# Four narrow projections with high and low weights side by side in one stationary operand

## The reference

```
aq, ak, av, bq, bkv, biq, bik, biw, cq, ck, cv, g = split_cols(u @ w_in[l])      # bik: 32 columns, biw: 8
s_idx = relu(einsum('bqhd,bkd->bqhk', iqb, ik)); score = einsum('bqhk,bqh->bqk', s_idx, iwb) * idx_scale
conv_val, conv_gate, z, xbc, dt = split(x @ even_w_in)                            # dt: 16 columns
q, k, v, g_out, g_low = split(x @ odd_w_in); log_g = log_sigmoid(g_low @ w_gate2 + b_gate) / 16   # g_low: 16 columns
```

## Time and profile before

| what | value |
|---|---|
| runs | 2524.91, 2529.27 and 7747.51 us, median 2529.27 |
| profiled execution, its own time | 2532.69 us |
| its span, first to last instruction | 2531.0 us |
| granted TensorE clock, mean | 0.997 |
| PE busy | 2479.7 us, 98%, 15181 matmuls |
| DVE busy | 1702.8 us, 67% |
| ACT busy | 1294.4 us, 51% |
| POOL busy | 405.1 us, 16% |
| HBM read | 247.99 MB, 99 GB/s over the span |

### The profile page before, as it was taken

One profiled execution on the slowest core, in us unless ns is written; L12 is line 12 of the kernel. 1 busy time (PEld: TensorE's weight loads), 2 busy tenths in 40 slices (PEclk: granted clock), 3 DMA queues, 4 the chain that ended last, 5 costly groups with the idle time before them and its releaser, 6 DMA issues.

```text
span 2531.0 us, 38409 instructions
## 1 busy us (share of the span) xinstructions
PE 2479.7 (98%) x15181; PEld 2158.2 (85%) x15181; DVE 1702.8 (67%) x3249; ACT 1294.4 (51%) x2558; POOL 405.1 (16%) x476
## 2 busy tenths in 40 slices
PE   7999999999999999999999999999999999999998
PEld 6876677899988978888897999889898897999888
DVE  5476977688863499997774988534735744988533
ACT  4365544367742435554654687424534453677422
POOL 2233342200000155543010100000000100100000
PEclk9999999999999999999999999999999999999999
DMA  9432234434443233212431343333321441333332
GB/s 285 134 93 71 66 99 125 131 94 125 117 128 98 77 100 100 59 59 92 126 87 48 91 116 111 92 96 86 90 78 34 127 132 53 89 110 108 92 98 86
DMA packets 455092, 253.29 MB, mean 100 GB/s; under 512 B 16458, under 2 KB 449310, under 8 KB 454911
## 3 DMA queue, kind: packets, MB, share of 16 engines
q1 hardware_dynamic: 451615, 243.18, 33.6%
q0 software_dynamic: 3152, 7.59, 1.3%
q10 hardware_dynamic: 144, 0.07, 0.0%
HBM read 247.99 MB, written 2.80 MB: 99 GB/s over the span
## 4 chain that ended last, share of the span: by engine, by line
PE 85%; DVE 9%; ACT 3%; issue 1%; DMA 1%; SPq 1%; POOL 0%; DVEq 0%; ACTq 0%; POOLq 0%
PE ps L1134 15%; PE ps L1142 15%; PE ps L1136 15%; PE ps L1199 4%; PE ps L1201 4%; PE ps L1204 4%; PE ps L1049 4%; PE ps L1051 4%; PE ps L1047 4%; PE ps L1375 1%; PE ps L1065 1%; PE ps L1718 1%; PE ps L1740 1%; PE ps L1067 1%; PE ps L1232 1%
## 5 line engine op out<-in xcount | busy, mean ns | idle before, releaser
L1948 ACT ACTIVATE wh<-w_f 128x512 fp32r<-128x512 f32 (+2 forms) x621 | 351.0, 614 | 337.1 <-PE ps L1142 157.1
L2912 DVE TENSOR_TENSOR w_r<-w_f,wh 128x512 fp32r<-128x512 f32 (+1 forms) x459 | 295.8, 688 | 334.5 <-ACT wh L1948 333.9
L1134 PE MATMUL ps<-XH,wh 128*128 128x512 f32 (+1 forms) x1136 | 457.9, 403 | 4.5 <-ACT wh L1948 3.5
L1136 PE MATMUL ps<-XL,wh 128*128 128x512 f32 (+2 forms) x1016 | 397.8, 392 | 0.2 <-DVE XL L3432 0.2
L1142 PE MATMUL ps<-XH,w_r 128*128 128x512 f32 (+2 forms) x1160 | 310.4, 391 | 1.0 <-DVE w_r L2912 0.8
L1136 PE MATMUL ps<-arena_r,wh 128*128 128x512 f32 (+1 forms) x808 | 296.5, 373 | 0.1
L4211 POOL TENSOR_TENSOR w_r<-w_f,wh 128x256 fp32r<-128x256 f32 (+1 forms) x314 | 236.3, 782 | 353.9 <-ACT wh L1948 353.7
L1134 PEld LDWEIGHTS ps<-XH,wh 128*128 128x128 f32 (+1 forms) x1136 | 211.8, 186 | 67.6 <-issue 15.1
L1142 PEld LDWEIGHTS ps<-XH,w_r 128*128 128x128 f32 (+2 forms) x1160 | 216.1, 186 | 51.4 <-DVE w_r L2912 3.2
L1136 PEld LDWEIGHTS ps<-XL,wh 128*128 128x128 f32 (+2 forms) x1016 | 189.3, 186 | 43.1 <-issue 1.9
L1134 PE MATMUL ps<-arena_r,wh 128*128 128x512 f32 (+1 forms) x568 | 210.2, 378 | 0.8 <-ACT wh L1948 0.8
(11 more groups left out here) (505 smaller groups left out, 5964.2 us busy)
## 6 DMA issues: line engine op xcount, KB each, us to landing
w_f<-in_mlp_w SPq DMA_DIRECT2D x126, 512.0 KB, 4.0
w_f<-in_w_ff SPq DMA_DIRECT2D x63, 512.0 KB, 4.1
w_f<-in_w_in SPq DMA_DIRECT2D x49, 512.0 KB, 3.8
w_f<-in_ada_w SPq DMA_DIRECT2D x35, 512.0 KB, 3.9
w_f<-in_even_w_in SPq DMA_DIRECT2D x35, 512.0 KB, 3.8
w_f<-in_odd_w_in SPq DMA_DIRECT2D x23, 512.0 KB, 3.8
w_f<-in_even_w_out SPq DMA_DIRECT2D x16, 512.0 KB, 4.0
w_f<-in_xa_w_v SPq DMA_DIRECT2D x16, 512.0 KB, 3.3
```

What stands on the lines that cost most here:

```text
L1134: e.matmul(b, hi[:, k, :], xh, start=u.first and k == 0, stop=False)
L1136: e.matmul(b, hi[:, k, :], xl, start=False, stop=False)
L1948: e.activation(high_flat(u)[:, s], flat(u, 0)[:, s], ACT.Copy).then_inc(act.sem, act.up("high", u.n, i))
L2912: e.tensor_tensor(low[:, s], raw_[:, s], high[:, s], ALU.subtract).then_inc(dve.sem, dve.up("low", u.n, i))
```

## The change

Where a projection has at most 40 columns, its high and its low weights are put beside each other in the 128 (or 64) columns of one stationary operand. One matmul then gives both products: of the high weights in the first half of the output rows, of the low weights in the second half. Two matmuls per chunk are left, by the high and by the low input, 16 a unit. (The product of low weights and low input is computed too.) The two halves are added later, by a product with a matrix that holds ones at both places.

- `ik` and `iw` become one unit `ikw` of 40 columns (32 and 8) that stand at 0 and at 64 of 128. It takes `ik`'s place (step 13 of differential attention). Its turn yields `iw`, and a second fp32 product with `ik_pick` yields `ik` four times; both at step 15, after that step's unit.
- `dt` stands at 0 and 32 of 64 columns; its turn is a product with `dt_pick` in place of a transpose.
- `low` stands at 0 and 32 of 64 columns; `wg2` holds its 16 rows twice, at partitions 0 and 32, with zeros between, and is loaded by two DMAs after a memset.
- The low part of these units is made by DVE. `ikw` and `dt` were POOL's before.
- One unit fewer is left for differential attention: `cq 0` moves to step 14, and every later unit up to `branch 1` moves up by one: index step 0 has `ck 1`, 1 `gate 0`, 2 `gate 1`, 3 `branch 0`, 4 `gate 2`, 5 `branch 1`. Block attention's step 0, which had `branch 1`, has none; from step 2 on the units are the ones of before.

```diff
+def side_by_side(name, dram, x, beside, wide):
+    u = Unit(name, 0, dram, x)
+    u.beside, u.wide = beside, wide
+    return u
...
-    ik = Unit("ik", 0, [w_in[:, COL_IK:COL_IK + IDX_DIM]] * 4, "X0")
-    iw = Unit("iw", 0, [w_in[:, COL_IW:COL_IW + 8]], "X0")
+    ikw = side_by_side("ikw", [w_in[:, COL_IK:COL_IK + IDX_DIM], w_in[:, COL_IW:COL_IW + 8]], "X0", 2 * IDX_DIM, 4 * IDX_DIM)
...
-        plans["diff", i] = [next(fill)] if i % 4 and i < 15 else []
-        plans["diff", i] += [next(qk)] if i >= 15 else []
+        plans["diff", i] = [next(fill)] if i % 4 and i < 14 else []
+        plans["diff", i] += [next(qk)] if i >= 14 else []
...
-        plans["moba", i] = [next(fill)] if i % 3 != 1 or i == 16 else []
+        plans["moba", i] = [next(fill)] if i and i % 3 != 1 or i == 16 else []
...
-    plans["ev gv"].insert(1, Unit("dt", 0, [even[:, EV_DT:EV_DT + SSM_HEADS]], "X3"))
+    plans["ev gv"].insert(1, side_by_side("dt", [even[:, EV_DT:EV_DT + SSM_HEADS]], "X3", 2 * SSM_HEADS, 4 * SSM_HEADS))
...
-    plans["gla low"] = [Unit("low", 0, [odd[:, OD_LOW:OD_LOW + GLA_RANK]], "X7")]
+    plans["gla low"] = [side_by_side("low", [odd[:, OD_LOW:OD_LOW + GLA_RANK]], "X7", 2 * GLA_RANK, 4 * GLA_RANK)]
...
-        u.low = "pool"
+        u.low = "dve" if u.beside else "pool"
...
+        def side(u, low):
+            a = high_slots[u.high][:, 0:KC * u.wide].rearrange("p (k c) -> p k c", k=KC)
+            return a[:, :, low * u.beside:low * u.beside + u.cols]
+        def standing(u, k):
+            return high_slots[u.high][:, k * u.wide:(k + 1) * u.wide]
...
-                        if u.name == "iw":
-                            last = e.matmul(b[:, j * 8:(j + 1) * 8], g[0:8, j * P:(j + 1) * P], ident[0:8, 0:8],
+                        if u.name == "ikw":
+                            w.wait_ge(dve, "ikw picks")
+                            last = e.matmul(b[:, j * 8:(j + 1) * 8], g[:, j * P:(j + 1) * P], iw_pick, start=True, stop=True)
+                        elif u.name == "dt":
+                            w.wait_ge(dve, "dt pick")
+                            last = e.matmul(b[:, j * 16:(j + 1) * 16], g[0:u.wide, j * P:(j + 1) * P], dt_pick[0:u.wide, :],
                                             start=True, stop=True)
-                        elif u.name == "dt":
-                            last = e.transpose(b[:, j * 16:(j + 1) * 16], g[0:16, j * P:(j + 1) * P], ident[0:16, 0:16])
+                    if u.name == "ikw":
+                        b, freed = att_now[0].take("ik")
+                        w.wait_ge(*freed)
+                        e.matmul(b[:, :], ik_pick, g, start=True, stop=True).then_inc(pe.sem, pe.up("ik turn"))
...
+            def wide_products(u):
+                b = bank_of(u)[0:u.wide, :]
+                after_long[0] = True
+                w.wait_ge(act, "high", u.n, 0)
+                w.wait_ge(dve, "low", u.n, 0)
+                for k in range(KC):
+                    xh, xl = chunk_of(u, k)
+                    w.wait_ge(act, "xh", u.x, k)
+                    e.matmul(b, standing(u, k), xh, start=k == 0, stop=False)
+                    w.wait_ge(dve, "xl", u.x, k)
+                    last = e.matmul(b, standing(u, k), xl, start=False, stop=k == KC - 1)
+                last.then_inc(pe.sem, pe.up("unit", u.n))
...
                 run(("diff", i))
+                if i == 15:
+                    flush()
...
-                e.matmul(b[:, :], wg2[0:GLA_RANK, hd * P:(hd + 1) * P], low[0:GLA_RANK, :], start=True, stop=True).then_inc(
+                e.matmul(b[:, :], wg2[0:4 * GLA_RANK, hd * P:(hd + 1) * P], low[0:4 * GLA_RANK, :], start=True, stop=True).then_inc(
...
+                        if u.beside:
+                            w.wait_ge(act, "high", u.n, 0)
+                            e.tensor_tensor(side(u, 1), chunks(flat(u, 0), u.kc, u.cols), side(u, 0).bitcast(F32),
+                                            ALU.subtract).then_inc(dve.sem, dve.up("low", u.n, 0))
+                            continue
...
+            e.tensor_tensor(ik_pick.rearrange("p (a b) -> p a b", a=4),
+                            ident[:, 0:IDX_DIM].unsqueeze(1).to_broadcast([P, 4, IDX_DIM]),
+                            ident[:, 2 * IDX_DIM:3 * IDX_DIM].unsqueeze(1).to_broadcast([P, 4, IDX_DIM]), ALU.add).then_inc(
+                dve.sem, dve.up())
...
-            e.dma_start(wg2[0:GLA_RANK, :], A["odd_w_gate2_2"][0]).then_inc(d_wg2.sem, d_wg2.up("wg2", by=16))
+            e.memset(wg2[0:4 * GLA_RANK, :], 0.0).then_inc(pool.sem, pool.up("wg2 zero"))
+            w.wait_ge(pool, "wg2 zero")
+            for r in (0, 2 * GLA_RANK):
+                e.dma_start(wg2[r:r + GLA_RANK, :], A["odd_w_gate2_2"][0]).then_inc(d_wg2.sem, d_wg2.up("wg2", by=16))
```

More of the change, by code:

```diff
@@ L246, in __init__ @@
         self.low, self.halved, self.k0 = "dve", apart, 0
+        self.beside = self.wide = None
         self.paired, self.high_after, self.shift = None, None, HALF_SHIFT
+def side_by_side(name, dram, x, beside, wide):
+    u = Unit(name, 0, dram, x)
+    u.beside, u.wide = beside, wide
+    return u
 class Step:
@@ L855, in program @@
                   ("xq", 0): qT, ("xq", 1): qT, "oq": q_, "ok": k_}
-        TURNED = ("iw", "dt")
+        TURNED = ("ikw", "dt")
+        ik_pick, iw_pick, dt_pick = lamb[:, P + 64:2 * P + 64], lamb[:, 2 * P + 64:2 * P + 72], soft[:, 48:48 + SSM_HEADS]
         RESIDUAL = {"wo": "r0", ("ff2", 0): "r1"}
@@ L1292, in run_units @@
                         group = [u, steps.pop(0)] if u.pair else [u]
-                        products(group)
+                        if u.beside:
+                            wide_products(u)
+                        else:
+                            products(group)
                         for v in group:
@@ L1946, in round_to @@
                             w.wait_ge(pe, "unit", u.high_before.n)
+                        if u.beside:
+                            e.activation(side(u, 0), chunks(flat(u, 0), u.kc, u.cols), ACT.Copy).then_inc(
+                                act.sem, act.up("high", u.n, 0))
+                            continue
                         for i, s in pieces(u, HIGH_PIECE):
@@ L1957, in flush @@
                     w.wait_ge(pe, "turn", u.name, u.m)
-                    if u.name == "iw":
+                    if u.name == "ikw":
                         copy(iw, b[:, 0:32].rearrange("p (a b) -> p a b", a=NT), "iw",
                              scale=IDX_HEADS ** -0.5 * IDX_DIM ** -0.5)
+                        w.wait_ge(pe, "ik turn")
+                        copy(ik, att_now[0].of("ik")[:, :], "ik", 0)
+                        att_now[0].free(act, "ik")
                     elif u.name == "dt":
@@ L2104, in evacuate @@
                     w.wait_ge(pe, "unit", u.n)
-                    copy(g[0:u.cols, 0:u.tokens], b, "turned", name, m)
+                    copy(g[0:u.wide, 0:u.tokens], lin.of(*u.out)[0:u.wide, 0:u.tokens], "turned", name, m)
                     lin.free(act, *u.out)
@@ L2108, in evacuate @@
                     turned.append(u)
-                elif name in ("kv", "ik", "low"):
+                elif name == "kv":
                     w.wait_ge(pe, "unit", u.n)
-                    copy({"kv": kvT, "ik": ik}.get(name, low[0:GLA_RANK, :]), b, name, m)
+                    copy(kvT, b, name, m)
+                    lin.free(act, *u.out)
+                elif name == "low":
+                    w.wait_ge(pe, "unit", u.n)
+                    copy(low[0:u.wide, :], lin.of(*u.out)[0:u.wide, :], name, m)
                     lin.free(act, *u.out)
@@ L3247, in vector_program @@
             e.tensor_scalar(gbh[:, :], columns("gate_b", 0, 24), 0.5, None, ALU.mult).then_inc(dve.sem, dve.up("gbh"))
+            e.tensor_tensor(ik_pick.rearrange("p (a b) -> p a b", a=4),
+                            ident[:, 0:IDX_DIM].unsqueeze(1).to_broadcast([P, 4, IDX_DIM]),
+                            ident[:, 2 * IDX_DIM:3 * IDX_DIM].unsqueeze(1).to_broadcast([P, 4, IDX_DIM]), ALU.add).then_inc(
+                dve.sem, dve.up())
+            e.tensor_tensor(iw_pick, ident[:, IDX_DIM:IDX_DIM + 8], ident[:, 3 * IDX_DIM:3 * IDX_DIM + 8], ALU.add).then_inc(
+                dve.sem, dve.up("ikw picks"))
             for i, part in enumerate(plans["project parts"]):
@@ L3683, in step_widths @@
                 fill(len(taps))
+            e.tensor_tensor(dt_pick, ident[:, 0:SSM_HEADS], ident[:, 2 * SSM_HEADS:3 * SSM_HEADS], ALU.add).then_inc(
+                dve.sem, dve.up("dt pick"))
             conv_taps("gv", "lead")
```

2 lines of the change are left out of this document (1 added, 1 removed).

## The result

The changed kernel took 2535.26 us, the median of 15 runs (2527.07 to 2542.16), the kernel before 2526.74 beside it: a ratio of **1.0025**, 95% interval 1.0014 to 1.0035. The forecast was 2528.2, 1.05 us less than the median of three runs that it started from (2529.27; one of the three took 7747.51). By the ratio the measurement is some 6 us more than before; the two medians are 8.5 us apart. Later the same kernel ran again on two other chips, with 1.0004 (0.9995 to 1.0013) and 1.0012 (1.0003 to 1.0021). So it is no faster: 1 us slower in one comparison, which isn't clear of nothing, and 3 and 6 us in the other two. Against two per cent that is no change, against the forecast the sign is wrong.

A forecast was written before the change was run, and what follows sets the result against it. TensorE, busy 98% of the span with 85% of the chain, was taken as the bound; attention stage +2.0, dt -1.2 and low -1.85 gave -1.05 us, 2528.2 us against the median 2529.3; range 2519 to 2534.

The forecast's parts named there:

- Price of a matmul: Narrow projections on TensorE: width is worth nothing, loads charged nothing; 16 wide matmuls for 24 narrow save 8 x 0.23 us.
- Differential attention: Up to the index scores: ikw saves 1.82 us, the extra turn costs 0.86, so the scores start 0.95 us earlier.
- The first wait: Index step 3: branch 0, one step earlier, makes TensorE wait 3.25 us for VectorE's low part of the fourth chunk.
- The second wait: Block attention's fifth scores: TensorE waits 3.5 us for ScalarE's copy of the first turned row, which frees the bank.
- The clock after a wait: After the two waits: one fall costs 1.7 us; stage taken at +2.0, bounds +0.35 (none) and +3.3 (both).
- dt and low: Even and gated mixers: dt -1.2 us (bounds 0 to -1.85), low -1.85 us (bounds 0 to -1.85).
- Sum: Whole kernel: +2.0 - 1.2 - 1.85 = -1.05 us, 2528.2 us; with the stage's bounds 2526.6 to 2529.5.
- VectorE as the bound with three falls: Block attention: falls after both waits and a third wait and fall at head 0's weighing; +2.05, 2531.3 us; chance 0.12.
- The whole saving: Attention stage: saving arrives whole if VectorE keeps up; stage -6.4, all -9.5, 2519.8 us; chance 0.15.
- only the first wait: Attention stage: VectorE makes good its lateness before the fifth scores; stage -3.15, all -6.2, 2523.1 us; chance 0.15.

The follow-up runs named there:

- e9: The changed kernel run again unchanged on another chip, for a second trace: 2528.82 us, 1.0004 of the kernel before.
- e3: Changed kernel, but no unit moves up: differential attention's step 14 has no unit, later units stand where they were before; 2527.86 us, 0.9993 of the kernel before.
- e8: Changed kernel with later units where they were before and 24 unused matmuls filling step 14; 2526.20 us, 0.9985 of the kernel before.
- e1: Kernel before with only dt and low side by side; index key, weights and all units as before; 2524.89 us, 0.9986 of the kernel before.
- e10: Early low part, early row copies and three moved searches, on the kernel before with only dt and low side by side; 2527.30 us, 0.9996.
- e2: Changed kernel, but VectorE makes differential attention's last low part at the end of index step 2, not in step 3; 2526.04 us, 0.9993 of before.
- f1: Changed kernel with 12 repeated matmuls in front of the first wait alone (branch 0); 2528.66 us, 0.9999 of the kernel before.
- f2: Changed kernel with 12 repeated matmuls in front of the second wait alone (branch 2); 2529.61 us, 1.0008 of the kernel before.
- e5: e2, with ScalarE copying turned rows ahead of the new row's exponentials in block attention's steps 2 to 4; 2525.98 us, 0.9984 of before.
- e7: e5, with three VectorE searches moved from block attention's steps 0, 2 and 4 to index step 1; 2520.48 us, 0.9972 of the kernel before.
- e11: e1, with VectorE's last differential-attention low part made three rows later, so that branch 0 waits; 2529.05 us, 1.0001 of the kernel before.
- f3: e7, with gate 4's high part and gate 3's evacuation on ScalarE ahead of the third row's exponentials; 2523.31 us, 0.9976 of before.
- f4: The changed kernel run a third time unchanged, beside f1 and f2 on their chip; 2531.78 us, 1.0012 of the kernel before.
- e4: e2, with the gap at block attention's step 14 and not its step 0, units after it moved up; 2529.81 us, 1.0003 of before.
- e6: Changed kernel with 12 repeated matmuls in front of each of the two long waits (branch 0, branch 2); 2527.07 us, 1.0001 of before.

## Why the prediction was wrong, step by step

- **Price of a matmul:** right. 16 wide matmuls of `dt` took 899.99 to 903.67 us, 0.23 each, of `low` 1783.65 to 1787.33. Their loads of 64 columns take 134 ns; the 128-column ones of `ikw` run at the same spacing. The packing rule of the Trainium skill weighed there (page "TensorE: Matmul & The Clock Gate", part on packing small matmuls) would have added an estimated 3.2 us; no stream here shows it. (That estimate priced the 64 columns as 128.)
- **Differential attention:** -0.14 for -0.95, a small miss. From the column sums in step 13 to the first index scores the kernel before takes 32.57 us (184.28 to 216.85), e9, with no fall there, 32.43 (181.92 to 214.35). The turns cost 1.07 more, 0.86 forecast. The rest isn't VectorE's low part of `ikw`: VectorE waited 1.73 us for ScalarE ahead of it, but had made that good by the next scores. It is POOL, which the sum put at nothing. POOL's low part of `cq 0` comes one unit earlier and now runs in step 13, 3.0 to 3.6 us long, where the kernel before has one piece of 0.32 us (`iw`, at 180.33). One operation of VectorE beside it takes some 0.5 us longer, 1.27 for 0.68 in e9. The scores of step 13 then wait for the sum behind it, and the products start 0.7 us later behind the column sums (2.8 for 2.13):

```profile
178.33 3.03 POOL L4279 TENSOR_TENSOR w_r<-w_f,wh 128x256 fp32r<-128x256 f32 x4 [12.95 <-ACT wh L1994]
180.64 1.27 DVE L2977 TENSOR_TENSOR arena_r<-arena_f,arena_r 128x512 fp32r<-128x512 f32 x1
181.92 1.10 PE L1344 MATMUL ps<-stat,ones 128*128 128x512 f32 x2 [1.40 <-DVE arena_r L2977]
...
184.00 0.70 PE L1415 MATMUL ps<-arena_f 64*128 64x256 f32 x2 [0.36 <-DVE modc L3184]
```

  e3 and e8 have that second wait too (0.24, 0.25), e1 and e10, where `iw` still stands ahead of `cq 0`, don't. In the changed kernel's first and third trace the clock also fell in step 13; it does in e1, without `ikw`, as well, so that is scatter.
- **The first wait:** right, 2.83 for 3.25; e2 removes it as its mechanism says. VectorE's subtraction took 0.68 us in all three traces, behind POOL's pieces and not beside them: the whole 0.55 came back where the sum had 0.3.
- **The second wait:** right, 3.14 for 3.5.
- **The clock after a wait: this is the step that failed.** I took a fall behind the first wait alone, +2.0 for the stage, and kept +3.3, for both, as a bound. In all three traces there was a fall behind each, in one two behind the second: 3.4, 5.1 and 3.4 us where the sum held 1.7. Over all runs the changed kernel has 5.2 us more clock time than before beside f1 and f2, and 3.5 more in e9's set. Without the clock the two stretches are +0.4, -0.1 and +0.4 us against before, and with differential attention the whole stage between -0.2 and +0.3, where the sum had +0.35.
- **Where the price of a fall came from.** It was read from one place of one trace, the wait of 2.79 us at 1137.81. That wait stands in all 17 traces, 2.78 or 2.79 us long, and a fall follows it in 9 of them. In the other 8, the changed kernel's first trace, e1, e2, e5, e7, e8, e11 and f3, the clock stays at 1.00; there TensorE comes early to the next chunk and waits another 0.5 us. So a fall behind a wait isn't certain, and one row couldn't tell. Here e1, without a fall, and e9, with one:

```profile
1137.32 0.50 PE L1706 MATMUL ps<-arena_r,wh 128*128 128x512 f32 x1 [2.79 <-ACT arena_r L2010]
1139.97 0.50 PE L1706 MATMUL ps<-arena_r,wh 128*128 128x512 f32 x1 [0.52 <-ACT arena_r L2010]
1130.00:1150.00 20.00, 16.69 (x58) 10.51 (x57) 16.22 (x26) 13.08 (x20) 0.00 (x0) 1.00 0.25 79
```

```profile
1139.90 0.50 PE L1711 MATMUL ps<-arena_r,wh 128*128 128x512 f32 x1 [2.79 <-ACT arena_r L2018]
1130.00:1150.00 20.00, 17.21 (x59) 11.11 (x58) 17.78 (x31) 13.14 (x20) 0.77 (x1) 0.91 0.23 79
```

  In the attentions all 11 waits of 2.76 to 3.63 us in 8 traces had a fall behind them, three of them two (e9, e2, e3).
- **dt and low:** right. From the first product of `dt` to the cumulated sum 26.68 us against 27.95, -1.27 for -1.2. `low` and its gate matmuls end 1.9 earlier. e1 has both together: -3.5, interval -0.8 to -6.
- **Sum:** with 5.2 for 1.7 of clock it is +2.4 us, 1.0010, where f4 measured 1.0012; with 3.5 it is +0.8, 1.0003, where e9 measured 1.0004. The first comparison's 1.0025 is 4 to 5 us more than these sums.
- **Rivals:** VectorE as the bound with three falls forecast +2.05, near in time. But its mechanism, a third wait at the weighing, isn't there; three falls came from two waits, in one of three traces. The whole saving and "only the first wait" fail at the 3.14 us before the fifth scores.

Still open: why one wait is followed by no fall, another by one or two, and why the first comparison came out 1.0025 and not nearer the other two; chip and run differ between them.

## What to carry to other kernels

Work taken off a nearly full TensorE in the middle of a pipelined stage leaves a gap, and the gap returns as waits on whichever engine feeds that stage; look first at what is queued ahead of the operation that ends the wait, since here reordering ScalarE and VectorE turned 1.0004 to 1.0025 into 0.9972. Charge every new wait of 3 us its length and a likely clock fall of 1.7 us of its own, not one fall for all; here 11 of 11 such waits in the attentions had one or two, and 9 of 17 at the same place in the even mixer. A few microseconds in 2500 can't be read from one trace: compare stretches between fixed instructions, take the clock's part out, and repeat.

## What the runs showed of the hardware beyond that

With the granted clock at 1.00 in both, the same 256-column matmuls ran at two paces in two runs of the same kernel: a mean of 281 ns each in the first trace, 276 in e9's, over 40 us near 1850 us.

```profile
L1264 PE MATMUL ps<-wh,XH 128*128 128x256 f32 x40 | 9.9, 281 | 0.0
```

```profile
L1264 PE MATMUL ps<-wh,XH 128*128 128x256 f32 x40 | 9.6, 276 | 0.0
```

Over the part behind `low` that is 742.1 us against 736.5, 5.6 us that no code makes; the profiled runs of the kernel before (742.2) and of e2 were of the slower kind, e4, e6 and e8 (736.4) of the other; e1 and e3 (740.6) and f2 (737.9) lie between. This alone is more than the change is worth.
